# A hybrid decoder layer on one core: two weight slabs loaded ahead of a wait, gate slabs split between the last recurrences, and GpSimd's key masks ahead of its waits for stores

## The reference

```python
mod = silu(c) @ w_ada + b_ada                     # shifts, scales, gates
h = rmsnorm(x) * (1 + sc1) + sh1
q, k, v, g, xr, gr = split(h @ w_in)
# retention: 4 heads, per sequence a state of 256 x 512
s_new = gamma ** C * s + (k * k_dec).T @ v        # also for the 8 samples
o = q k^T-scores @ v + (q @ s) * q_dec            # then group norm, * silu(g)
# RG-LRU: 12 tiles of 128 channels
xc = causal_conv(xr);  r, i = sigmoid(xc @ w_a), sigmoid(xc @ w_x)
a = exp(-8 r softplus(-lru));  h_t = a h_{t-1} + sqrt(1 - a^2) i xc
rnn_y = h_t * gelu(gr)
mixed = (ga * (ret_y @ w_br_ret) + gb * (rnn_y @ w_br_rnn)) @ w_out
x = x + g1 * rmsnorm(mixed);  then a SwiGLU FFN in the same manner
```

## Time and profile before

| | us |
|---|---|
| three runs | 1448.87, 1449.13, 1451.73 (median 1449.13) |
| profiled execution, its own time | 1449.33 |
| its span, first to last instruction | 1447.5 |
| TensorE matmuls busy | 1377.7 (95%) |
| VectorE, ScalarE, GpSimd busy | 717.9, 484.3, 181.3 |
| chain that ended last, share of TensorE | 82% |
| mean granted TensorE clock | 0.979 |

### The profile page before, as it was taken

How to read it: one execution, slowest core, us unless ns; L and a number is a source line. 1 busy time by engine, 2 the same in 40 slices (tenths; PEclk the granted TensorE clock), 3 DMA queues, 4 the chain that set the end, 5 groups by cost and what they waited for, 6 DMA issues and landing times.

```text
span 1447.5 us, 23984 instructions
## 1 busy us (share of the span) xinstructions
PE 1377.7 (95%) x10324; PEld 1281.7 (89%) x10324; DVE 717.9 (50%) x998; ACT 484.3 (33%) x683; POOL 181.3 (13%) x284
## 2 busy tenths in 40 slices
PE   6699999899999899999999999999799999999995
PEld 3599999788997798799889879999799999999995
DVE  4349888522242475267437624966743333332225
ACT  4277778312231231232224123336422222212221
POOL 1013222000113212212320322000000000000000
PEclk8899999999999999999999999999899999999998
DMA  8422222475424434434442443243022222222321
GB/s 340 149 70 73 74 88 74 171 283 180 159 81 147 154 103 132 163 97 141 148 166 67 138 159 133 88 162 120 0 73 88 88 88 88 88 83 81 88 87 62
DMA packets 49930, 172.70 MB, mean 119 GB/s; under 512 B 5537, under 2 KB 7713, under 8 KB 49569
## 3 DMA queue, kind: packets, MB, share of 16 engines
q1 hardware_dynamic: 39456, 135.51, 28.1%
q0 software_dynamic: 9216, 33.56, 6.6%
q10 hardware_dynamic: 1152, 2.10, 0.4%
HBM read 149.82 MB, written 21.32 MB: 118 GB/s over the span
## 4 chain that ended last, share of the span: by engine, by line
PE 82%; DVE 9%; ACT 3%; DMA 3%; issue 2%; POOL 0%; SPq 0%; DVEq 0%; ACTq 0%; POOLq 0%
PE ps L760 66%; PE ps L769 3%; PE ps L1005 2%; PE ps L1016 2%; PE ps L808 1%; PE ps L988 1%; PE ps L1048 1%; PE ps L1034 1%; DMA raw<-in_w_brnn 1%; PE ps L891 1%; DMA raw<-in_w_out 1%; DVE w_lo L1517 1%; DMA raw<-in_w_rnn 1%; DVE x_res L1872 1%; DVE rsn L1867 1%
## 5 line engine op out<-in xcount | busy, mean ns | idle before, releaser
L760 PE MATMUL ps<-h_hi,w_hi 128*128 128x272 f32 x2096 | 444.1, 293 | 22.8 <-ACT xs L1287 9.5
L760 PE MATMUL ps<-h_hi,w_lo 128*128 128x272 f32 x2096 | 436.3, 290 | 0.0
L760 PE MATMUL ps<-h_lo,w_hi 128*128 128x272 f32 x2096 | 435.3, 289 | 0.0
L1517 DVE TENSOR_TENSOR w_lo<-raw,w_hi 128x1024 fp32r<-128x1024 f32 (+2 forms) x190 | 226.5, 1195 | 335.3 <-ACT w_hi L1189 332.9
L760 PEld LDWEIGHTS ps<-h_hi,w_hi 128*128 128x128 f32 x2096 | 333.9, 190 | 36.6 <-issue 18.0
L760 PEld LDWEIGHTS ps<-h_lo,w_hi 128*128 128x128 f32 x2096 | 332.4, 190 | 0.0
L760 PEld LDWEIGHTS ps<-h_hi,w_lo 128*128 128x128 f32 x2096 | 330.2, 190 | 0.0
L1189 ACT ACTIVATE w_hi<-raw 128x1024 fp32r<-128x1024 f32 (+2 forms) x190 | 195.6, 1030 | 355.9 <-PE ps L760 241.5
L1791 DVE SCALAR_TENSOR_TENSOR state<-state,ps 128x512 f32<-128x512 f32 x64 | 41.1, 684 | 111.1 <-PE ps L1048 110.9
L760 PE MATMUL ps<-a_hi,w_hi 128*128 128x272 f32 x308 | 63.8, 288 | 2.1 <-DVE a_lo L1526 2.1
L760 PE MATMUL ps<-a_hi,w_lo 128*128 128x272 f32 x308 | 63.8, 288 | 0.0
(11 more groups left out here) (238 smaller groups left out, 1848.8 us busy)
## 6 DMA issues: line engine op xcount, KB each, us to landing
raw<-in_w_head SPq DMA_DIRECT2D x48, 512.0 KB, 3.8
raw<-in_w_fin SPq DMA_DIRECT2D x38, 512.0 KB, 3.4
state<-in_state POOLq DMA_DIRECT2D x32, 512.0 KB, 4.1
out_rs<-state POOLq DMA_DIRECT2D x32, 512.0 KB, 3.9
raw<-in_w_rnn SPq DMA_DIRECT2D x24, 512.0 KB, 3.5
ada_more<-in_w_ada SPq DMA_DIRECT2D x23, 512.0 KB, 6.2
ada_raw<-in_w_ada SPq DMA_DIRECT2D x16, 512.0 KB, 14.6
raw<-in_w_bret SPq DMA_DIRECT2D x16, 512.0 KB, 3.5
```

Source lines behind the costliest of these rows:

```text
L760: mm = nc.tensor.matmul(dst[:, half, :], a, b[:, half * HALF:(half + 1) * HALF], start=first and j == 0, stop=last and j == 2)
L1517: V.tensor_tensor(lo[:, 0:cols], raw_slab(i)[0][:, 0:cols], hi[:, 0:cols].bitcast(F32), ALU.subtract).then_inc(lo_ready, 1)
```

## The change

Three edits. SP's list gets a call that issues the slabs `xr 1` and `gr 1` ahead of its wait for `h`. At n = 11 VectorE splits one more gate slab after the recurrence of tile 9 and one after that of tile 10, instead of one after tile 10 and one after tile 11. GpSimd's turn masks the keys and stores state u - 1 first, and waits for the store of state u - 2 and loads state u + 2 last.

```diff
@@ SP
                 sp.dma_start(ada_raw[:, n, :], w["w_ada"][n // KD, n % KD]).then_inc(ada_in[n], 16)
+            load_to(pl.slab[("gr", 1, "w", 0)])
             sp.wait_ge(h_ready, KD)
             sp.wait_ge(c4_ready, 1)
             sp.dma_start(rg_w[:], w["w_rg"]).then_inc(rg_in, 16)
@@ VectorE
                 ahead(("gr", n))
-                for i in recurrences_at(n):
+                gate_slabs = list(GATE_TILES.get(n, ()))
+                last_turns = recurrences_at(n) + (recurrences_at(NR) if n == NR - 1 else ())
+                for i in last_turns:
                     decays(i)
                     recur(i)
-                for m in GATE_TILES.get(n, ()):
+                    if n == NR - 1 and i < NR - 1:
+                        ahead(("gb", gate_slabs.pop(0)))
+                for m in gate_slabs:
                     ahead(("gb", m))
-                    if n == NR - 1 and m == GATE_TILES[n][0]:
-                        for i in recurrences_at(NR):
-                            decays(i)
-                            recur(i)
@@ GpSimd
                 for b in range(NB):
                     u = h * NB + b
-                    if STATES <= u + 2 < H * NB:
-                        last = u + 2 - STATES
-                        pool.wait_ge(s_stored[last % STATES], 16 * (last // STATES + 1))
-                        load_state(u + 2)
                     if u >= 2:
...
                     if u:
                         store_state(u - 1)
+                    if STATES <= u + 2 < H * NB:
+                        last = u + 2 - STATES
+                        pool.wait_ge(s_stored[last % STATES], 16 * (last // STATES + 1))
+                        load_state(u + 2)
```

## The result

The changed kernel takes 1468.62 us (median; 1466.47 to 1470.26), the kernel before 1449.56 beside it (1448.87 to 1451.73): a ratio of 1.0128, 95% interval 1.011 to 1.0146. It is 19 us slower; the forecast was 9.5 us faster. The profiled execution took 1469.21 us with a span of 1467.4 and a mean granted clock of 0.970.

The account below looks back on a forecast made before the run. TensorE, 95% of the span, was taken as the bound, with its waits as the target. -11.3 + 2.1 - 4.5 + 4.2 = -9.5 us gave a 1438.0 span, 1439.6 as median; own range 1437.5 to 1441.8, wider 1433.5 to 1443.8.

Parts of the forecast that it names:

- Edit 1: At `xr 1`: early slabs remove 9.46 us of waiting and 1.82 of low clock, 11.3 us faster; bounds 9.5 to 11.8.
- Rival (d): At `gr 1` or `gb 0`: the first wait only moves, 4 us of waiting and 1.5 of clock, 1445; chance 0.06.
- Edit 2: From `gb 6` to `bn 1.1`: 5.3 us won become a 7.2 us wait plus low clock, 2.1 us slower in all.
- Rival (a): At `bn 1.1`: earlier issue makes the weights land in time, so 1432.2; chance 0.1.
- Edit 3, the gain in head 0: At `b7` of head 0: earlier masks save 2.8 us of waiting plus low clock, 4.5 us faster.
- Edit 3, the late loads: Heads 1 to 3: state loads behind stores make TensorE wait 1.2 us at `p1`, 0.2 at `p3`; 4.2 us, bound 7.5.
- The load's data stand behind its data: At `p1` of head 1: the load lands behind the store's landing at 565.2, at 565.9 to 566.5.
- rival (e): At the six state waits: loads landing 6.7 us after issue cost 2.8 us each, slower than before; at 3 each 1453; chance 0.03.
- Rival (b): At the state loads: the store is no obstacle and states are in time, 1435.4; chance 0.12.
- (c): Heads 1 to 3: the state waits reach their upper bound of 7.5 us, 1442.9; chance 0.13.
- The Trainium skill's price: For GpSimd transfers: 3.2 us per state, so the `p1` load lands at 564.3, before TensorE asks; edit 3 all gain.

Follow-up runs that it names:

- e1: Kernel before with only slabs `xr 1` and `gr 1` issued ahead of SP's wait for `h`: 1438.67 us, ratio 0.9922.
- e3: Kernel before with only GpSimd's new order (masks, store, then load): 1473.9 us, ratio 1.0162.
- e12: Kernel before with the early `xr 1` and `gr 1` slabs and VectorE's earlier gate-slab splits, GpSimd unchanged: 1439.73 us, ratio 0.993.
- e13m: Kernel before with the early `xr 1` and `gr 1` slabs and GpSimd's order masks, load, store: 1433.08 us, ratio 0.9888.
- load_first: Changed kernel with GpSimd's load of state u + 2 ahead of the store, both still behind VectorE's update: 1449.67 us, ratio 0.9997.
- after_gap: Changed kernel with 2.2 us of spare GpSimd work between store and load: 1474.56 us in one profiled execution.
- after_tiny: Changed kernel storing only 16 rows of 128 floats per state, output incomplete: 1444.82 us in one profiled execution.
- after_small: Changed kernel storing only a quarter of each state row, output incomplete: 1444.53 us in one profiled execution.

## Why the prediction was wrong

**Edit 1: right.** Forecast -11.3. `e1` is 11.2 faster by its medians. In single traces mark A came 9.2 to 11.6 earlier than in the profile of before, since the start itself varies by a microsecond either way: over the eleven runs with the edit A has a mean of 62.0, over the two without (before and `e3`) 73.3. The wait for `xr 1` is gone, and nothing at `gr 1` or `gb 0` took its place. Rival (d) is out.

**Edit 2: right in sign and path, off in one size.** Forecast: waits of 0.8, 2.8 and 7.2, `bn 1.1` started 0.2 earlier, 2.3 of low clock, +2.1 in all. Measured in `e12`: 1.08, 2.44 and 4.17, and B to C longer by 1.6, if the kernels with edit 2 and an unsplit burst (mean 159.9) are held against those without (158.3). The last wait is shorter than forecast for two reasons. The wait of 2.44 us lowered the clock too, 6.26 us for 36 matmuls, which takes 1.5 us out of the later wait at no cost; and the slab was landed at 283.3, which against A is 1.6 us earlier than in the kernel before. Rival (a) is out: measured from mark A `bn 1.1` is issued 3.7 us earlier, but takes 13.24 us.

**Edit 3, the gain in head 0: the mechanism is right, the gain was eaten.** The wait for the masks of `b7` is gone from the changed kernel. But ahead of it stands the wait of 2.79 us for `p3`, which the forecast put at 0.2 and hid; there is another of 0.74 for `p2`, and the next slab takes 7.71 us (at 476.90 in the chain), 1.7 more than at full clock. That is 5.2 us against a gain of 5.3 as `e13m` shows it without the loss (4.5 forecast), and C to D is unchanged (-0.1).

**Edit 3, the late loads: this term failed.** The prediction said "three heads, 4.2 us", with 7.5 as its bound; it was 27.2. Two things were wrong in it.

The first is the landing. For `p1` the forecast put it 5.7 to 6.3 us after the store's issue (565.9 to 566.5 against 560.21). In heads 1 to 3 it was 7.2, 6.6 and 6.4. "The load's data stand behind its data" held, for the load landed 1.2 to 1.8 us behind the store. In head 1 the store itself took 6.0 us instead of 5.0; that was not the load's doing, since in heads 2 and 3 stores with the same load behind them took 4.8 and 4.7, against 4.8 and 5.3 before. What is special in head 1 is that SP issued its slab 0.29 us behind the store instead of 0.58, and that the slab's packets went first. Why they did is open.

For `p3` the error was larger. The forecast used the store's 3.4 us, which is the time of a store with nothing else going on, and that store still took 3.3. But the changed kernel issues its store at 601.52, its load at 602.29 and a slab from SP at 602.89, and the load shares the engines with the slab: it lands 7.7 us after the store's issue, and 7.2 and 7.3 in heads 2 and 3, where 4.8 to 5.4 were forecast. From the load's issue to its landing SP's whole slab went through, and 1.57 MB in all:

```profile
q0 software_dynamic: 288, 1.05, 50.2%
q1 hardware_dynamic: 144, 0.52, 20.8%
```

The median wait was so 1.95 us at `p1` and 2.66 at `p3`, not 1.2 and 0.2, and the six sum to 14.7: 6.5 at `p1` where 3.6 were forecast, 8.2 at `p3` where 0.6 were. A load after its store had no row in the old trace. The nearest was not taken: at 375.05 GpSimd issued four loads back to back beside a full stream from SP, and the trace of the kernel before shows how long each took in the median:

```profile
state<-in_state POOLq DMA_DIRECT2D x4, 512.0 KB, 8.4
```

It would have put the upper bound of a load at 8.4 us instead of some 5.5, and rival (e) needed 6.7. It got 3 in 100 because "none near them in the trace took more than 5.0". That reading was slightly off, a store at 824.73 took 5.3; and those transfers had at most one other beside them, where this one goes out with two.

The second is the clock. The forecast let waits of 1.0 to 1.6 us keep the clock, which held at that size in all places but one. Its bound (7.5) added only 0.9 us a head beyond that, and rival (e) priced its waits alone. The other 12.5 of the 27.2 us are low clock: slabs of 8.19, 8.37, 8.36 and 8.43 us where 6.21 is usual are 8.5 of it, and the rest lies in the matmuls between wait and slab, as in the row `610.49 1.84`, which took 0.97 in `load_first`. Four of the six waits cost it, those of 2.85, 3.04, 2.51 and 2.66; those of 1.95 and 1.72 did not, nor did one of 2.34 in `after_gap`, behind which a slab took 6.22. `after_tiny` and `load_first`, with no wait over 1.8 us in heads 1 to 3, show no slow slab there. `after_small` shows that size is not all: behind a wait of 1.34 us a slab took 7.74.

**The rivals.** What happened is rival (e)'s mechanism at nearly its size in waiting (2.5 each, not 2.8) and with the clock on top. Rival (b), the store is no obstacle, is out, and (c), at 7.5 us, was too low. The Trainium skill's price for a GpSimd transfer (DMA: Bandwidth & Descriptors, section Anatomy of one DMA, SWDGE (gpsimd) path) gives an estimate of 3.2 us for a state. The traces disagree: single loads took 3.9 us at least, and 4.6 even behind a quarter of a store.

**What stays open.** The traces show that at both places of the changed kernel the slab's 0.52 MB move inside the late load's time; without a run that leaves the slab out, its share of the lateness is not shown apart from the store's. Open too is why packets are so slow when such a cluster begins (180 GB/s with the engines full), and why SP's slab went ahead of an earlier store in head 1. The clock's cost is measured, but not what decides whether a wait lowers it.

## What to carry to other kernels

A transfer that is moved behind another one has to be timed from the moment both are issued with all that the other queues issue then. Its own length in quiet is no guide, nor is that of the transfer ahead of it: ask which row of the trace has as many bytes in flight, and bound by that one. When an instruction is moved so that something else no longer waits, look at what it now waits for itself. Here the load moved behind masks, which cost it nothing, and behind a store that waits for VectorE, which cost everything; the order masks, load, store keeps the whole gain. And price a new wait on TensorE with the clock behind it: in this kernel, waits of 2.5 to 3.0 us cost some 3 us more each.

## What the runs showed of the hardware

- A state load from GpSimd takes 3.9 us at least and 4.1 in the median before, 4.6 to 5.3 us when issued 0.8 us behind a store of a quarter of the bytes, and 5.6 to 6.9 us 0.8 us behind a store of 512 KB, with a weight slab beside them in each case (heads 1 to 3).
- Issuing the load 3.0 us after the store instead of 0.8 brings it back to 4.0 us, and it lands as late against the store's issue in head 1 (7.0 and 7.2 us).
- A slab of SP issued 0.29 us behind GpSimd's store went first: 48 packets from 553 to 555, and none of the store's.
- While such a cluster begins, the engines can be busy and move little: the first row has 0.73 of their time and 98 GB/s. In the changed kernel, with busy times, clock, DMA share and GB/s as above:

```profile
553.00:555.00 2.00, 2.00 (x19) 2.00 (x17) 0.72 (x1) 0.00 (x0) 1.76 (x5) 1.00 0.73 98
555.00:557.00 2.00, 1.76 (x13) 1.32 (x11) 0.60 (x1) 0.61 (x1) 0.56 (x1) 1.00 0.93 344
```

- Behind waits of nearly the same length TensorE's clock fell or did not. There was no loss behind 1.72, 1.95 and 2.34 us, and 1.7 to 2.2 us in the next slab behind 2.51, 2.66, 2.79, 2.85 and 3.04 (the changed kernel) and 1.2 to 1.6 behind 2.53, 2.61, 2.69 and 2.71 (`after_gap`). But behind one of 1.34 us in `after_small`, at 866.83, the clock fell as well, and not before the slab had begun. The rows have PE busy, clock, DMA share and GB/s around it:

```profile
866.00:868.80 2.80, 1.97 (x11) 1.00 0.27 107
868.80:877.00 8.20, 8.20 (x52) 0.79 0.20 66
```
